# Feed-forward in two phases: seven block products for gate and up, activations through DRAM, resident down weights

## The reference

```python
x = x + rmsnorm(mix, norm_mix_post)
hf = rmsnorm(x, norm_ffn_pre)
ff = (jax.nn.silu(hf @ w_gate) * (hf @ w_up)) @ w_down
x = x + rmsnorm(ff, norm_ffn_post)
```

## Time and profile before

| | |
|---|---|
| median of 3 runs | 3634.64 us (3631.37 to 3636.22) |
| the profiled execution's own time | 3640.15 us |
| its span | 3638.4 us |
| feed-forward, from its first transfer to the end | 1608 us, from 2030 |
| TensorE busy | 3078.1 us (85%) |
| VectorE, ScalarE, GpSimd busy | 41%, 33%, 5% |
| granted TensorE clock, mean | 0.95 |
| DMA traffic | 428.85 MB, mean 118 GB/s |

### The profile page before, as it was taken

The page is one execution under the profiler, slowest core; times in us unless marked ns, Lnnn a source line. Parts: engine busy times, 40 slices in busy tenths (PEclk is TensorE's granted clock), DMA queues, the critical chain, the costliest instruction groups (busy, mean ns, idle before and its releaser), DMA issues. The chain is left out here.

```text
span 3638.4 us, 58850 instructions
## 1 busy us (share of the span) xinstructions
PE 3078.1 (85%) x23798; PEld 2751.8 (76%) x23798; DVE 1500.7 (41%) x2849; ACT 1217.7 (33%) x1912; POOL 184.6 (5%) x167
## 2 busy tenths in 40 slices
PE   0499999924888877736499699999999999999998
PEld 0499999903777766613388599999999999999897
DVE  4300000044666767622244334533544544444554
ACT  3211111104666766601344222322322322322333
POOL 4200000000000000000011000100100100000100
PEclk9999999967999999967799799999999999999999
DMA  2111121114211122089454533433433433433454
GB/s 98 64 70 70 70 71 46 46 18 138 64 42 51 44 63 72 21 263 332 149 157 150 180 126 121 157 136 122 168 133 132 162 133 128 166 133 123 160 188 147
DMA packets 176501, 428.85 MB, mean 118 GB/s; under 512 B 14952, under 2 KB 100512, under 8 KB 155808
## 3 DMA queue, kind: packets, MB, share of 16 engines
q1 hardware_dynamic: 154920, 399.40, 32.7%
q10 hardware_dynamic: 21392, 26.82, 2.1%
HBM read 361.45 MB, written 64.71 MB: 117 GB/s over the span
## 5 line engine op out<-in xcount | busy, mean ns | idle before, releaser
L1601 ACT ACTIVATE ffn_wdh<-ffn_wdr 128x1024 fp32r<-128x1024 f32 x132 | 139.9, 1060 | 923.8 <-PE ffn_py L1580 923.8
L172 PE MATMUL ffn_pg<-ffn_hh,ffn_wgh 128*128 128x384 f32 (+1 forms) x1056 | 347.5, 329 | 36.0 <-DVE ffn_wgl L1671 36.0
L174 PE MATMUL ffn_pg<-ffn_hh,ffn_wgl 128*128 128x384 f32 (+1 forms) x1056 | 346.8, 328 | 0.0
L173 PE MATMUL ffn_pg<-ffn_hl,ffn_wgh 128*128 128x384 f32 (+1 forms) x1056 | 346.3, 328 | 0.0
L173 PE MATMUL ffn_pu<-ffn_hl,ffn_wgh 128*128 128x384 f32 (+1 forms) x1056 | 343.7, 326 | 0.0
L172 PE MATMUL ffn_pu<-ffn_hh,ffn_wgh 128*128 128x384 f32 (+1 forms) x1056 | 343.7, 326 | 0.0
L174 PE MATMUL ffn_pu<-ffn_hh,ffn_wgl 128*128 128x384 f32 (+1 forms) x1056 | 343.7, 326 | 0.0
L1671 DVE TENSOR_TENSOR ffn_wgl<-ffn_wgr,ffn_wgh 128x2048 fp32r<-128x2048 f32 x132 | 313.3, 2374 | 71.9 <-ACT ffn_wgh L1595 71.9
L1676 DVE TENSOR_TENSOR ffn_wdl<-ffn_wdr,ffn_wdh 128x1024 fp32r<-128x1024 f32 x132 | 161.6, 1224 | 416.3 <-ACT ffn_wdh L1601 416.3
L1579 PE MATMUL ffn_py<-ffn_wdl,ffn_ah 128*128 128x512 f32 x748 | 293.1, 392 | 0.0
L1580 PE MATMUL ffn_py<-ffn_wdh,ffn_al 128*128 128x512 f32 x748 | 293.1, 392 | 0.0
(11 more groups left out here) (203 smaller groups left out, 5982.5 us busy)
## 6 DMA issues: line engine op xcount, KB each, us to landing
ffn_wgr<-in_w_gu SPq DMA_DIRECT2D x132, 1024.0 KB, 4.8
ffn_wdr<-in_w_dn SPq DMA_DIRECT2D x132, 512.0 KB, 3.2
att_raw<-out_zT SPq DMA_DIRECT2D x64, 256.0 KB, 2.9
str_kr<-in_cache_ak SPq DMA_DIRECT2D x8, 2048.0 KB, 18.5
str_vr<-in_cache_av SPq DMA_DIRECT2D x8, 2048.0 KB, 15.5
out_zT<-prj_zo ACTq DMA_DIRECT2D x64, 224.0 KB
prj_raw<-in_w_slab SPq DMA_DIRECT2D x12, 1024.0 KB, 5.0
out_v<-prj_vo ACTq DMA_DIRECT2D x68, 128.0 KB, 1.8
```

Of the source, the lines that this page charges most:

```text
L172: nc.tensor.matmul(out, a_hi(k), b_hi(k), start=(k == 0), stop=False)
L173: nc.tensor.matmul(out, a_hi(k), b_lo(k), start=False, stop=False)
L174: last = nc.tensor.matmul(out, a_lo(k), b_hi(k), start=False, stop=(k == kk - 1))
```

## The change

feed_forward becomes two functions with a DRAM tensor act_t (128 x 22 x 2176) between them.

gate_up takes the tokens in 3 passes (724, 724 and 728 tokens), each cut into two halves of 362 (364) tokens, and K into two halves of 512. With a11, a12 the two halves of K of the first tokens, a21, a22 those of the second, and b11, b21 (gate), b12, b22 (up) the two halves of K of the weights of one j, gate and up of both token halves come out of seven products of block sums instead of eight of blocks. A unit (p, j) is 7 products x 4 chunks of K x 3 matmuls of 362 columns, 84 matmuls; there are 66 units. The sums of the weights (tr) are made by GpSimd, those of the tokens (sr, and a21 in place) once a pass, by VectorE and GpSimd in the first pass and by GpSimd in the others. ScalarE and VectorE split all seven blocks of weights (3.5 K elements a partition) instead of four. The products land in eight banks (X, Y, Z, W, twice) and are combined by five VectorE additions (u2, u3, c22, c21, c12). The raw weights wr and the sums tr have one buffer each, wh and wl two.

down_out computes the down product with 34 units of 66 matmuls of 512 columns: for each half c of the outputs, 22 x 512 columns of split weights stay resident (wh, wl), and 17 tiles of 128 tokens pass by; their activations (ar, one buffer) are read back from act_t and split, once for each c. The first half's results wait in ys, the second half's finish the row: squares, rms, scaling, residual, store, tile by tile.

```diff
-def feed_forward(nc, t, keep):
-    NBL = (NT + 2) // 3
-    TM = 3 * P
...
+TWIN = [(0, 362), (724, 362), (1448, 364)]
+def gate_up(nc, t, keep, act_t):
...
+        wr = m.sb("wr", [P, 2, KD, P])
+        tr = m.sb("tr", [P, 4, HK, P])
+        wh = [m.sb(f"wh{u}", [P, NX, HK, P], F32R) for u in range(2)]
+        wl = [m.sb(f"wl{u}", [P, NX, HK, P], F32R) for u in range(2)]
...
+                def weights(n):
...
+                    if n >= 1:
+                        sp.wait_ge(s_wl, 3 * n)
+                        sp.wait_ge(s_t, 4 * n)
+                    sp.dma_start(wr[:], t["w_gu"][n % NJ]).then_inc(l_w, 16)
...
+                for n in range(NU):
+                    p, j = divmod(n, NJ)
+                    weights(n + 2)
+                    if j == 2 and p + 1 < len(TWIN):
+                        hidden(p + 1)
+                    store(n)
...
+                def w_sums(n):
...
+                    pool.wait_ge(l_w, 16 * (n + 1))
+                    if n >= 1:
+                        pool.wait_ge(s_wl, 3 * (n - 1) + 2)
+                    nc.gpsimd.tensor_tensor(tr[:, 1], b22, b12, ALU.subtract).then_inc(s_t, 1)
+                    pool.wait_ge(s_t, 4 * n + 1)
+                    nc.gpsimd.tensor_tensor(tr[:, 0], tr[:, 1], b11, ALU.add).then_inc(s_t, 1)
+                    pool.wait_ge(s_t, 4 * n + 2)
+                    nc.gpsimd.tensor_tensor(tr[:, 3], b21, tr[:, 0], ALU.subtract).then_inc(s_t, 1)
+                    pool.wait_ge(s_t, 4 * n + 3)
+                    nc.gpsimd.tensor_tensor(tr[:, 2], b12, b11, ALU.subtract).then_inc(s_t, 1)
...
+                for n in range(NU):
+                    w_sums(n + 1)
+                    if j == 4 and p + 1 < len(TWIN):
+                        h_sums(p + 1)      # four sums of 128 x 4*362
...
+                def product(n, x):
+                    out = {0: X, 1: Y, 2: Z, 3: X, 4: W, 5: Z, 6: W}[x][u][:, :w]
...
+                    if x == 3:
+                        pe.wait_ge(s_p1, n + 1)
...
+                    if x == 5:
+                        pe.wait_ge(s_add, 5 * n + 2)           # u3 of this unit
+                    if x == 6:
+                        pe.wait_ge(s_wl, 3 * n + 3)
+                        pe.wait_ge(s_add, 5 * n + 3)           # c22
...
+                for n in range(NU):                            # scalar
+                    high_gate(n + 1)       # 1024 elements, waits for the load
+                    act.wait_ge(s_pr, NX * n + 1)
+                    nc.scalar.activation(p1[:, :w], X[u][:, :w], ACT.Copy).then_inc(s_p1, 1)
+                    if end: high_h(p + 1, 0)
+                    high_sums(n + 1)       # 2048 elements, waits for all of w_sums(n + 1)
+                    if end: high_h(p + 1, 1); high_h(p + 1, 2)
+                    high_up(n + 1)         # 512 elements
+                    nc.scalar.activation(sg[:, :w], X[u][:, :w], ACT.Silu).then_inc(s_g1, 1)
...
+                    nc.scalar.activation(c21[:, :w], c21[:, :w], ACT.Silu).then_inc(s_g2, 1)
...
+                for n in range(NU):                            # vector
+                    low_gate(n + 1)
+                    nc.vector.tensor_tensor(u2[:, :w], p1[:, :w], Y[u][:, :w], ALU.add).then_inc(s_add, 1)
+                    low_sums(n + 1)
+                    nc.vector.tensor_tensor(u3[:, :w], u2[:, :w], Z[u][:, :w], ALU.add).then_inc(s_add, 1)
+                    low_up(n + 1)
...
+def down_out(nc, t, keep, act_t):
...
+                def weights(q):
...
+                    if q >= 4:
+                        sp.wait_ge(s_wl, q - 3)
+                    sp.dma_start(wr[q % 4][:], t["w_dn"][j][:, c * HALF:(c + 1) * HALF]).then_inc(l_w[q % 4], 16)
+                def acts(n):
...
+                    if n >= 1:
+                        sp.wait_ge(s_al, n)
+                    sp.dma_start(ar[:], act_t[:, :, i * P:(i + 1) * P]).then_inc(l_a, 16)
...
+                high_a(0)                                      # scalar
+                for j in range(NJ):
+                    high_w(j)
+                high_a(1)
+                for n in range(NM):
+                    if n >= 1:
+                        high_a(n + 1)
+                    if n == NT - 1:
+                        for q in range(NJ, 2 * NJ):
+                            high_w(q)      # waits until TensorE has read block j for the last time
+                    squares(n)
...
+def feed_forward(nc, t, keep):
+    act_t = nc.dram_tensor("mid_act", (P, NJ, TOK), F32, kind="Internal").ap()
+    gate_up(nc, t, keep, act_t)
+    down_out(nc, t, keep, act_t)
```

More of the change, by code:

```diff
@@ L1447, in _ @@
                         hidden(x - 2)
-def feed_forward(nc, t, keep):
-    NBL = (NT + 2) // 3
-    TM = 3 * P
-    assert NJ % 2 == 0 and NT % 3 == 2
-    with ExitStack() as ctx:
[L1459 to L1511, removed]
@@ L1517, in _ @@
             def _(sp):
[L1518 to L1535, removed]
@@ new lines, in hidden, with store @@
+                def hidden(p):
+                    t0, w = TWIN[p]
+                    if p >= 1:
+                        sp.wait_ge(s_hl, NX * p)
+                    sp.dma_start(hr[:, :, :2 * w], t["hT"][:, :, t0:t0 + 2 * w]).then_inc(l_h, 16)
+                def store(n):
+                    p, j = divmod(n, NJ)
+                    t0, w = TWIN[p]
+                    sp.wait_ge(s_a, 2 * n + 2)
+                    sp.dma_start(act_t[:, j, t0:t0 + 2 * w], ao[n % 2][:, :2 * w]).then_inc(st[n % 2], 16)
@@ L1645, in _, with high_gate @@
-                walk(act, step, lambda b: sums(b - 1), nothing, lambda b: hidden(b + 1), evict)
-                sums(NBL - 1)
+                def high_gate(n):
+                    if n >= NU:
+                        return
+                    u = n % 2
+                    act.wait_ge(l_w, 16 * (n + 1))
+                    if n >= 2:
+                        act.wait_ge(s_pr, NX * (n - 1))
+                    nc.scalar.activation(plain(wh[u]), wr[:, 0].rearrange("p (a k) c -> p a k c", a=2), ACT.Copy).then_inc(s_wh, 1)
@@ L1723, in _, with low_w, low_a @@
-                hidden(0)
-                split_gate(0, 0, 0)
-                split_down(0, 0, 0)
-                walk(dve, step, nothing, lambda b: scaled(b - 1), lambda b: hidden(b + 1), evict)
-                scaled(NBL - 1)
+                def low_w(q):
+                    c, j = divmod(q, NJ)
+                    dve.wait_ge(s_wh, q + 1)
+                    nc.vector.tensor_tensor(wl[:, j, :], wr[q % 4][:], f32(wh[:, j, :]), ALU.subtract).then_inc(s_wl, 1)
+                def low_a(n):
+                    if n >= NM:
+                        return
+                    dve.wait_ge(s_ah, n + 1)
+                    nc.vector.tensor_tensor(al[n % 2][:], ar[:], f32(ah[n % 2][:]), ALU.subtract).then_inc(s_al, 1)
@@ new lines, in _ @@
+                low_a(0)
+                for j in range(NJ):
+                    low_w(j)
+                low_a(1)
+                dve.wait_ge(s_g, 16)
+                for n in range(NM):
+                    if n >= 1:
+                        low_a(n + 1)
+                    if n == NT - 1:
+                        for q in range(NJ, 2 * NJ):
+                            low_w(q)
+                    evict(n)
+                    if n >= NT:
+                        finish(n - NT)
+def feed_forward(nc, t, keep):
+    act_t = nc.dram_tensor("mid_act", (P, NJ, TOK), F32, kind="Internal").ap()
+    gate_up(nc, t, keep, act_t)
+    down_out(nc, t, keep, act_t)
```

517 lines of the change are left out of this document (370 added, 147 removed).

## The result

The changed kernel takes 3758.05 us (median of 4 runs, 3754.54 to 3765.21) where the kernel before takes 3633.97 in the same comparison: a ratio of 1.0343, 95% interval 1.033 to 1.0356, 124 us slower. The forecast was 3794, with 3690 to 3905.

The account below looks back on a forecast made before the run. The prediction took TensorE's own pace to bound the feed-forward before and the weight round to bound gate_up after; 1182 + 585 = 1767 against 1608 us, 159 more, gave 3634.6 + 159 = 3794 us, range 3690 to 3905.

Parts of the forecast that it names:

- step 1: Gate and up matmuls: an eighth of the columns goes, 66 units take 911 us instead of 1042, worth 131 us.
- Step 2, the circle of the weights: gate_up: single-buffered load, sums, splits, u3 and low_up close a round of 17.0 us against TensorE's 13.8.
- The handover of 0.2: In the round, SP sees the semaphore and issues the weight load: 0.2 us, an own estimate.
- The contention term: In the round, GpSimd's four sums lose 0.9 us beside VectorE's low_gate, taking 6.3 us.
- The bounds of the round: 15.8 us without contention and with the quickest load; 18.6 with all sums at the shared pace and a 5.0 load.
- The 211 us: gate_up: TensorE stands 3.2 us in each of 66 rounds, waiting for u3 before product 5.
- Step 3, the ends of gate_up: Start 27, 65 rounds 1105, changes of pass and token sums 28, end 22: gate_up takes 1182 us.
- Step 4, down_out: Matmuls 514, start 37, change of half 15, tail 10, handover 3, finish and stores 6: 585 us.
- The circle of ar: down_out: activation load 8, high_a, low_a and handovers take 13.9 us, just under TensorE's unit of 15.1.
- The circle did not hide: Judges the rival that gate_up's weight round takes no more than 13.8 us and TensorE binds: 3572 us, chance 8%.
- The low clock: Rival: gate_up pauses halve TensorE's clock; nearly free at 3 us each, 3980 with 3 us more a round; chance 5%.
- Down was not bound by its loads: Judges the rival that activation loads of 10.5 us make a down_out unit 16.4 us: 44 us more, 3838, chance 5%.

Follow-up runs that it names:

- e7: Changed kernel without any sums of weights, the splits reading the unsummed blocks (part of the calculation left out): 3556.94 us, ratio 0.9786.
- e6: Changed kernel with gate_up rewritten as eight plain block products, no sums, weights and hidden rows double-buffered, down_out untouched: 3664.04 us, ratio 1.0089.
- e1: Changed kernel with VectorE making u3 before low_sums instead of behind it: 3727.62 us, ratio 1.0254, round 16.20 us.
- e2: Changed kernel with GpSimd making the fourth sum a second time and high_sums waiting for it: 3860.92 us, ratio 1.0625, round 18.26 us.
- e10: Changed kernel with three idle GpSimd operations a unit, made after the four sums and outside the round: 3765.43 us, ratio 1.0363, round 16.84 us.
- e4: Changed kernel with the four sums of the weights made by VectorE before low_gate instead of by GpSimd: 3586.18 us, ratio 0.9868, round 13.95 us.
- e8: Changed kernel with u3 first, b12 and b11 summed first, weights loaded in two transfers, three quarters early: 3574.48 us, ratio 0.9833.
- e3: Changed kernel with low_gate cut to 8 of 1024 columns from the third unit on: 3708.18 us, ratio 1.0207, round 15.93 us.

## Why the prediction was right, step by step

**What bounds, and step 1.** Right. TensorE's pace in the unit is 0.165 a matmul (forecast 0.1641), a hidden round gives 13.92 to 13.95 (forecast 13.8). The eighth of the columns is saved; e7, run beside e6, shows what it is worth when nothing stands before it: 107 us of the 131, where the rounds, 13.92 instead of 15.87, make up 127 and longer starts and changes of pass take 20 back.

**Step 2, the circle of the weights.** Right in every member and shown by taking one out (e1, -0.60 for 0.52), adding one (e2, +1.46 for 1.4 to 1.6), adding the same work outside it (e10, +0.04) and removing it as the bound in three ways (e4, e7, e8). The round measured 16.8 where 17.0 was forecast: the sums took 6.6 rather than 6.3, the load with its handover, u3 and the other handovers less. The handover of 0.2 in front of the load had no row behind it; low_up ends at 2605.90 and the load is issued at 2605.93. The contention term was 0.9 and e3 gives 0.87 for low_gate, but the prediction held low_gate alone to blame: in all the sums lose some 1.3 us, and the rest stands beside the activation products. The bounds of the round, 15.8 and 18.6, come to 16.0 and 18.7 when their own terms are added up, which changes nothing here. The 211 us that were to be spent in TensorE's pauses appear as 146 us of waiting for u3 and some 45 us lost to half clock (28 stretches of 1.6).

**Step 3, the ends of gate_up.** From the first transfer to the load behind low_up of unit 0: 25.9 (forecast 27). Over the 64 rounds that follow, 3148.79 - 2050.84 = 1098 are 23 more than 64 x 16.80; 28 was forecast for these losses, all at the changes of pass and around the token sums, which took some 19; the first rounds, which the forecast left out, took 3. One more round of 16.8 leads to the last low_up. From the last low_up to the first transfer of down_out 25.5 (22 + 3). In all 1166 us against 1185. The 1.67 us for an operation of 1448 elements was right (1.65 to 1.67 where GpSimd does not disturb it), but not by the rows named: a line through 3358 ns for 3072 and 2374 for 2048 gives 1.80.

**Step 4, down_out.** 3755.9 - 3191.1 = 565 against 582 without the handover. The circle of ar stayed under TensorE's unit, as taken: its load was 7.5 (forecast 8, with bounds 6.7 and 10.5), and units start 14.96 apart (15.1). The start lost 31 instead of 37, for the second unit starts at 3237.05, 46 us after the first transfer and not 52. At the change of half TensorE waited 3.9 us for weights and 6.0 for activations, 10 instead of 15. From its last matmul, at 3747.1, to the end are 9 us (10); the 6 us given to the stores in front of low_a did not show. The second and the nineteenth unit, each behind a pause, ran at half clock at first and took 16.65 and 17.08 us; these 4 us were not in the sum, and the shorter units made up for them.

**Sum.** 1166 + 565 = 1731 against 1767. With the first transfer at 2024.9 instead of 2030 (among the variants, whose earlier stages are the same, it lies between 2019.9 and 2029.3, so this is no effect of the change) the 159 us of the forecast become 118 in the spans and 124 in the medians. No term was off by more than 20 us, but most were a little high, so they added up to a forecast 35 us above the measurement, over a quarter of the change itself. That the contention was put too low and the handovers and u3 too high is chance, and it helped the round.

**The rivals.** The circle did not hide. The low clock came, in 28 stretches over the 66 units, mostly at pauses shorter than the one of the earlier trace rows, and cost next to nothing, as its rival's first half said: with 1.6 us of low clock TensorE's own time is 15.5 us, still below the round of 16.8. The Trainium skill, TensorE: Matmul & The Clock Gate, Part 1, describes a loop whose waits for transfers, some 3 to 5 us long, throttle the clock in every turn. The trace agrees only in part: the pauses here are 2.58 us long, and behind many of them the clock stayed. Down was not bound by its loads.

## What to carry to other kernels

Before work is removed from the busiest engine, follow every single-buffered tile once around: load, each operation that reads it in turn with the engine that issues it, release, and add up the durations. If that sum is longer than the new, shorter time of the busiest engine, the tile sets the pace, and the sum is the forecast for one unit. Then the cure is not at the wait that the profile shows on the busiest engine; shorten or leave the circle anywhere (a faster engine for one member, a part of the load issued earlier, an operation ahead of the chain instead of in it), and stop when the sum is below the busiest engine's time, for after that the same edits bring nothing.

## What the runs showed of the hardware

- Two-input SBUF operations of VectorE and GpSimd slow each other: in the round shown VectorE's 1024-element subtraction took 2.32 us instead of 1.2 and its 362-element product 1.62 instead of 0.53, GpSimd's 512-element sum up to 2.16 instead of 1.26. The times look as if one waited for the other to end: low_gate ends at 2616.35, 1.1 us behind the end of L1551, and L1553, started meanwhile, ends 1.15 behind low_gate. This is read from one round and not tested. VectorE's addition with one input in PSUM (L1754) never took more than 0.534 us in 66 times, though it falls beside the sums.
- Pauses of TensorE of 2.58 us were followed by half clock (0.52 over 3.5 us) in some rounds and by the full clock in others (the one that ends at 2722.89), in a loop that kept it busy for the other 14 us; behind pauses of 1.0 to 1.4 us the clock stayed.
- 1408 KB read from DRAM in pieces of 512 bytes landed in 7.5 us, 1536 KB in pieces of 1536 bytes in 7.3, about a tenth less in the same time. The prediction's dearer bound for it, 10.5 us, was far off.
